# One reciprocal-root activation for Ln and Exp, and a Newton step of three operations, in a hybrid decoder block on one core

## The chip, the core and the metric

The kernel runs on one core of one Trainium2 chip. The core has five engines that run side by side, each with an in-order queue of its own: TensorE (PE: matmuls, transposes), VectorE (DVE), ScalarE (ACT: activations, copies, some DMA issues), GpSimd (POOL: here it splits weights and issues gathers) and SyncE (SP: issues the weight loads). They meet only at semaphores. The metric is the device time of one execution in microseconds, taken as the median over runs.

## The reference

One decoder block over 1024 tokens of width 1024, in float32: a root-mean-square norm, projections, retention in 4 heads with a variance norm inside each head, a short convolution, a gated merge, an expert retrieval over 16,384 experts behind a second norm, a gated per-layer input behind a third, and a final norm.

```python
def rms_norm(x, g):
    y = xf * lax.rsqrt(jnp.mean(xf * xf, axis=-1, keepdims=True) + EPS)
    return (y * g).astype(x.dtype)

def head_group_norm(y):
    mu = jnp.mean(y, axis=-1, keepdims=True)
    yc = y - mu
    return yc * lax.rsqrt(jnp.mean(yc * yc, axis=-1, keepdims=True) + EPS)

a = rms_norm(h, g_mix);  proj = a @ w_in
ret = silu(g_ret) * head_group_norm(chunkwise_retention(q, k, v))
merged = sigmoid(gate_r) * (ret @ w_ret_up) + sigmoid(gate_c) * ((cb * z) @ w_conv_up)
h = h + merged @ w_out
h = h + peer_ffn(rms_norm(h, g_ffn), ...)
h = h + sigmoid(rms_norm(h, g_ple) @ w_ple_gate) * (p @ w_ple_proj)
out = rms_norm(h, g_final)
```

## The kernel before

Activations are held transposed (channels on the 128 partitions, tokens along the free dimension). Every float32 matmul is made of three (high times high, high times low, low times high), so each operand is split: a cast gives the high half and a subtraction the low half. For weights POOL does both (`split`, L645 and L647) in the early part of the program, one pair of instructions for each weight tile of 128x1024, as soon as PE has finished the tile before the last; later ACT casts and POOL subtracts (L653). For activations ACT casts, and DVE and POOL share the subtractions.

The tokens go through the mixers in two passes: pass 0 has 384 tokens, pass 1 has 640. In each pass `mixers` runs four heads (`head`; each is six weight tiles on PE, with the work of the head before in between), a last `head` that only finishes, then the gate, convolution and merge tiles, and the output tiles. After the mixers comes the norm ahead of the query tiles (norm 1 in pass 0, norm 3 in pass 1). Norm 0 stands at the start of the program, norm 2 (pass 1's first) runs beside pass 0's query tiles. Then the experts: 128 tiles against `peer_u`, 128 groups of rows against `peer_v`, with gathered rows dotted on DVE beside them. The tail is the projection of the per-layer input (`ple_part`, 8 parts on PE), norm 4 in two halves of 512 tokens, 16 gate tiles (t = 0 to 15, `F_TILE + t`) and the final norm, half by half.

Each of the 16 roots is made alike. PE sums squares against a matrix of equal numbers into a scratch bank of PSUM (L792, L1088 in the tail), so every partition holds the mean. ACT takes Ln(mean + eps) (L1114; L1542 and L1568 in the tail) and then Exp(-0.5 x) (L1116; L1545, L1570), which is the rough root in `nt0`. DVE refines it once by Newton (`newton`; `half_rstd` in the tail): L1606 makes -0.5 (mean + eps) from the scratch bank while Exp is still to come and thereby drains the bank, L1609 squares the root, L1611 multiplies the two, L1612 adds 1.5 and multiplies by the root (L2242, L2244, L2246 and L2247 in the tail). Then the rows are scaled: L1624 for norms, L1884 and L1887 for a head, L2253 and L2278 in the tail.

Roots by place: norms 0 to 3 (4), heads of pass 0 (4), heads of pass 1 (4), norm 4 (2 halves), final norm (2 halves). In `head`, ACT's queue holds behind the root the copies of the transposed values (L1195, L1198, L1200) and the sigmoids (L1205, L1207). Ahead of norm 4's second half stands its first, and behind both stand the copies `ple_out(1)` and later (L1534), which free the PSUM banks that PE's parts 3 and later wait for:

```python
ple_out(0)
act.wait_ge(stat_filled, 5)
row_std(0)
row_std(1)
for n in range(1, 4):
    ple_out(n)
```

ACT evaluates functions from tables, and an ACT_TABLE_LOAD stands in its queue wherever the next function is not in the set that is loaded. Ln, Exp and Sigmoid each have one in front of them here.

Of the kernel before, what the change touches and what calls it, by code (L numbers as in the profile page):

```python
# [31 lines left out]
P = 128  # L32
# [10 lines left out]
EPS = 1e-6  # L43
LOWEST = -3.0e38
# [228 lines left out]
def build(nc, x_t, p_t, stream, u_rows, v_rows, key_t, gains, conv_c, rope, head_c, shape_c, out_t,  # L273
          score_d, act_d, gate_d, res_d):
    with ExitStack() as ctx:
# [35 lines left out]
        eps_t = lay("eps_t", [P, 1], F32)  # L311
        headz = lay("headz", [P, 2], F32)
# [450 lines left out]
        def _(pe):  # L763
# [65 lines left out]
            def head(h, ps, first=False):  # L829
# [24 lines left out]
                if not first:  # L854
                    pe.wait_ge(ysqsum_ready, heads)
                    column_mean(m, "var", ones_v, nt2[ps], WIDTH[ps])
# [30 lines left out]
            def mixers(ps):  # L887
# [15 lines left out]
                def variance():  # L903
                    pe.wait_ge(ysqsum_ready, HEADS * ps + HEADS)
                    column_mean(m, "var", ones_v, nt2[ps], WIDTH[ps])
# [199 lines left out]
        def _(act):  # L1105
# [6 lines left out]
            def rough_rstd(ps, slot, done, count):  # L1112

                act.activation(nt0[ps][:, :], slot[:, 0:(TS, TDN, T)[ps]], ACT.Ln, bias=eps_t[:, 0:1]).then_inc(done, 1)  # L1114
                act.wait_ge(done, count + 1)
                act.activation(nt0[ps][:, :], nt0[ps][:, :], ACT.Exp, scale=-0.5).then_inc(done, 1)  # L1116

            def norm_std(norm, ps, slot):
                act.wait_ge(stat_filled, norm + 1)
                rough_rstd(ps, scr[slot], std_done, 2 * norm)  # L1120
# [42 lines left out]
            def head(h, ps, first=False, last=False):  # L1163
# [26 lines left out]
                if not first:  # L1190
                    act.wait_ge(scr_filled, m.filled("var"))
                    rough_rstd(ps, scr[1], gstd_done, 2 * (heads - 1))
# [371 lines left out]
            def out_std(half):  # L1564
# [3 lines left out]
                act.activation(n0, scr[half][:, 0:HALF], ACT.Ln, bias=eps_t[:, 0:1]).then_inc(std_done, 1)  # L1568
                act.wait_ge(std_done, 2 * (6 + half) + 1)
                act.activation(n0, n0, ACT.Exp, scale=-0.5).then_inc(std_done, 1)  # L1570
# [19 lines left out]
        def _(dve):  # L1590
# [23 lines left out]
            def norm_rstd(norm, ps, slot):  # L1614
                newton(ps, scr[slot], std_done, 2 * norm + 2, stat_drained, norm + 1)
# [219 lines left out]
            def head(h, ps, first=False, last=False):  # L1835
# [40 lines left out]
                if not first:  # L1876
# [5 lines left out]
                    newton(ps, scr[1], gstd_done, 2 * heads, scr_drained[1], m.drained("var"))  # L1882
# [32 lines left out]
            def mixers(ps, spare):  # L1915
# [3 lines left out]
                if ps == 0:  # L1919
                    with dve.Fori(1, HEADS) as h:  # L1920
                        inside = steps.enter(h - 1, 6 + 3 + 2 + 2)
# [316 lines left out]
            def half_rstd(turn, half, mean):  # L2238
                at = slice(half * HALF, (half + 1) * HALF)
                n0, n1, n2 = nt0[2][:, at], nt1[2][:, at], nt2[2][:, at]  # L2240
                dve.wait_ge(std_done, 2 * (turn + half) + 1)
                dve.tensor_scalar(n1, mean, -0.5, -0.5 * EPS, ALU.mult, ALU.add).then_inc(stat_drained, 1)  # L2242
# [149 lines left out]
```

## Time and profile before

| | us |
|---|---|
| median of 3 runs | 3545.93 (3545.28 to 3547.4) |
| the profiled execution | 3540.74 |
| its span | 3538.9 |
| PE busy | 3391.1 (96%) |
| DVE busy | 2532.9 (72%) |
| POOL busy | 2175.7 (61%) |
| ACT busy | 1287.8 (36%) |
| mean granted share of TensorE's clock | 0.983 |

The span is the time from the first instruction to the last in one profiled execution; 1.84 us of that execution lie around it. Times in the rows are counted from the start of the span. A row of a timeline has the start, the duration, the engine, the line, the operation, output<-inputs and the shapes; in brackets stands how long the engine was idle before it and who ended that. Several instructions of one kind in a row are merged (x2, x3).

### The profile page before, as it was taken

How to read it: one execution, taken by the hardware profiler on the slowest of the kernel's cores; microseconds unless marked ns; L12 is line 12 of the kernel's file. 1: busy time of each engine (PE TensorE's matmuls, PEld its weight loads, DVE VectorE, ACT ScalarE, POOL GpSimd, SP SyncE). 2: the span in 40 equal slices, each digit the busy share in tenths (PEclk: the TensorE clock that was granted, in tenths of full speed). 3: DMA queues.
4: the chain of work that ended last, by engine and by line, in shares of the span. 5: the costliest groups of instructions: out<-in, count | busy, mean ns of one | idle time of the engine just before them, and what ended most of it. 6: DMA issues, size and time to landing. Idle time of an engine off the chain costs nothing.

```text
span 3538.9 us, 58475 instructions
## 1 busy us (share of the span) xinstructions
PE 3391.1 (96%) x22379; PEld 3332.5 (94%) x22379; DVE 2532.9 (72%) x4232; ACT 1287.8 (36%) x2013; POOL 2175.7 (61%) x1426
## 2 busy tenths in 40 slices
PE   7899989998999989999999999999999999999987
PEld 6899979988999979999999999999999999999975
DVE  5615467668887667898989899754667676767567
ACT  3310131232121232456565655653333333333242
POOL 5578865332678656566666666765566665666544
PEclk9999989999999999999999999999999999999998
DMA  4233432111589868789898988988999998999712
GB/s 153 81 116 122 136 114 79 57 50 60 184 311 316 279 218 310 252 306 335 306 331 309 328 313 311 319 299 284 337 318 334 341 321 304 320 333 320 271 48 95
DMA packets 324309, 851.18 MB, mean 241 GB/s; under 512 B 27665, under 2 KB 125457, under 8 KB 320785
## 3 DMA queue, kind: packets, MB, share of 16 engines
q0 software_dynamic: 110592, 402.70, 31.2%
q1 hardware_dynamic: 92160, 300.62, 25.6%
q10 hardware_dynamic: 121360, 145.25, 12.2%
q8 instruction: 122, 2.00, 0.2%
q14 instruction: 75, 0.61, 0.0%
HBM read 756.20 MB, written 92.27 MB: 240 GB/s over the span
## 4 chain that ended last, share of the span: by engine, by line
PE 84%; DVE 10%; ACT 2%; issue 2%; DMA 1%; POOL 1%; ACTq 0%; DVEq 0%; SPq 0%; POOLq 0%
PE main L777 53%; PE main L1037 24%; PE scr L975 4%; DMA rows<-v_rows,s_idx 1%; DVE rows L1800 1%; PE scr L875 1%; PE scr L792 1%; DVE rowb L1624 1%; PE main L1079 1%; PE scr L816 0%; DVE res L2286 0%; DVE y L1884 0%; PE scr L820 0%; DVE rowb L2010 0%; DVE rowb L1600 0%
## 5 line engine op out<-in xcount | busy, mean ns | idle before, releaser
L653 POOL TENSOR_TENSOR w_lo<-raw,w_hi 128x1024 fp32r<-128x1024 f32 x206 | 534.3, 2594 | 421.9 <-ACT w_hi L1132 417.9
L777 PE MATMUL main<-mix_hi,w_hi 128*128 128x320 f32 (+1 forms) x2816 | 685.2, 317 | 29.8 <-DVE mix_lo L1632 9.9
L777 PE MATMUL main<-mix_lo,w_hi 128*128 128x320 f32 (+1 forms) x2816 | 673.2, 313 | 0.0
L777 PE MATMUL main<-mix_hi,w_lo 128*128 128x320 f32 (+1 forms) x2816 | 673.1, 313 | 0.0
L1807 DVE SCALAR_TENSOR_TENSOR scr<-rows,s_dot,scr 128x1024 f32<-128x1024 f32 x381 | 489.0, 1284 | 167.0 <-DMA rows<-v_rows,s_idx 150.6
L777 PEld LDWEIGHTS main<-mix_hi,w_hi 128*128 128x128 f32 x2816 | 476.8, 190 | 34.5 <-issue 19.6
L777 PE MATMUL main<-a_hi,w_hi 128*128 128x320 f32 (+1 forms) x1728 | 465.8, 324 | 24.2 <-DVE a_lo L1632 8.6
L686 POOL DMA_INDIRECT rows<-u_rows,s_idx x384 | 397.4, 1035 | 135.8 <-issue 69.0
L777 PEld LDWEIGHTS main<-mix_lo,w_hi 128*128 128x128 f32 x2816 | 480.3, 189 | 0.0
L777 PEld LDWEIGHTS main<-mix_hi,w_lo 128*128 128x128 f32 x2816 | 479.5, 189 | 0.0
L1037 PE MATMUL main<-h_hi,v_hi 128*128 128x320 f32 x2048 | 467.7, 310 | 9.3 <-issue 3.5
L1800 DVE CUSTOM_DVE_ANT_0 rows<-rows,scr 128x1024 f32<-128x1024 f32 x384 | 446.1, 1215 | 41.4 <-PE main L777 22.7
L1037 PE MATMUL main<-h_lo,v_hi 128*128 128x320 f32 x2048 | 467.4, 309 | 0.0
L1037 PE MATMUL main<-h_hi,v_lo 128*128 128x320 f32 x2048 | 467.0, 309 | 0.0
L733 POOL TENSOR_TENSOR v_lo<-raw,v_hi 128x1024 fp32r<-128x1024 f32 x126 | 301.8, 2415 | 264.3 <-ACT v_hi L1429 257.9
L777 PE MATMUL main<-a_lo,w_hi 128*128 128x320 f32 (+1 forms) x1728 | 458.9, 320 | 0.0
L777 PE MATMUL main<-a_hi,w_lo 128*128 128x320 f32 (+1 forms) x1728 | 458.3, 320 | 0.0
L686 POOL DMA_INDIRECT rows<-v_rows,s_idx x384 | 368.9, 961 | 126.8 <-issue 82.9
L1037 PEld LDWEIGHTS main<-h_hi,v_hi 128*128 128x128 f32 x2048 | 342.5, 188 | 10.5 <-issue 4.0
L1037 PEld LDWEIGHTS main<-h_hi,v_lo 128*128 128x128 f32 x2048 | 343.0, 188 | 0.0
L1037 PEld LDWEIGHTS main<-h_lo,v_hi 128*128 128x128 f32 x2048 | 343.0, 188 | 0.0
L777 PEld LDWEIGHTS main<-a_hi,w_hi 128*128 128x128 f32 x1728 | 302.9, 190 | 32.6 <-issue 19.0
(270 smaller groups left out, 5137.4 us busy)
## 6 DMA issues: line engine op xcount, KB each, us to landing
raw<-stream SPq DMA_DIRECT2D x480, 512.0 KB
gate_d<-gbuf ACTq DMA_DIRECT2D x20, 2048.0 KB, 8.9
act_d<-actb ACTq DMA_DIRECT2D x120, 320.0 KB
gate_in<-gate_d ACTq DMA_DIRECT2D x30, 1280.0 KB
h<-act_d SPq DMA_DIRECT2D x120, 320.0 KB
rows<-u_rows,s_idx POOLq DMA_INDIRECT x384
rows<-v_rows,s_idx POOLq DMA_INDIRECT x384
score_d<-stage ACTq DMA_DIRECT2D x16, 320.0 KB
```

The source lines that it names most:

```text
L653: pool.tensor_tensor(w_lo[:, s, :], raw[:, s, :], w_hi[:, s, :].bitcast(F32), ALU.subtract) \
L686: pool.indirect_dma_start(rows[HOMES[k]][:, :], None, table[:, :], bass.IndirectOffsetOnAxis(ap=s_idx[:, t, n:n + 1], axis=0)) \
L733: pool.tensor_tensor(v_tile(v_lo, n), raw[:, n % 2, :], v_tile(v_hi, n).bitcast(F32), ALU.subtract).then_inc(v_split, 1)
L777: last = pe.matmul(main[s][:, dst:dst + n], wt[:, s, c * P:(c + 1) * P], rows[:, c, src:src + n], start=(c == 0 and wt is w_hi and rows is ...
L792: last = pe.matmul(slot[:, at:at + n], ones[:, :], src[:, at:at + n], start=True, stop=True)
L875: last = pe.matmul(slot[:, t * P:(t + 1) * P], qrow[ps][:, s, t * P:(t + 1) * P], row_of(keys[ps], 2 * h + s), start=True, stop=True)
L975: last = pe.matmul(scr[1][:, w * HALF + k * P:w * HALF + (k + 1) * P], hot_key(half + w, 1, k), hot_key(half + w, 0, k), start=True, stop= ...
L1037: last = pe.matmul(slot[:, half * HALF:half * HALF + HD], v_tile(vt, n)[:, col:col + P], ht[u][:, k, half * HD:(half + 1) * HD], start=(k ...
L1079: last = pe.matmul(main[s][:, half * HALF:(half + 1) * HALF], wt[:, n // 4, col:col + P], pt[:, c, half * HALF:(half + 1) * HALF], start=( ...
L1624: dve.scalar_tensor_tensor(rowb[ps][:, c % 4, :], res_row(c, ps), gain[:, which, c:c + 1], nt0[ps][:, :], ALU.mult, ALU.mult).then_inc(row ...
L1800: dve.tensor_tensor_reduce(got[:, :], got[:, :], acc[:, :], 1.0, 0.0, ALU.mult, ALU.add, s_dot[:, t, n:n + 1]).then_inc(dot_done, 1)
L1807: dve.scalar_tensor_tensor(acc[:, :], got[:, :], s_dot[:, t, n:n + 1], acc[:, :], ALU.mult, ALU.add).then_inc(dot_done, 1)
```

## The change

Ln and Exp become one activation, Abs_reciprocal_sqrt, which reads the scratch bank with a scale and a bias. The matrix of ones that sums squares now holds -1/D, so the bank holds minus the mean; the scale turns the sign back and divides by a constant (ROOT, ROOT_V for the heads) so that Newton's step needs no halving. DVE's step is then: square the root; (bank - eps) times that square, which reads the bank and drains it; add a constant and multiply by the root. The early instruction L1606 and L2242 is gone. The semaphores of the root count one for each root instead of two.

```diff
+ROOT = 0.5 ** (2 / 3)
+ROOT_V = 2.0 ** (2 / 3)
...
-                    column_mean(m, "var", ones_v, nt2[ps], WIDTH[ps])
+                    column_mean(m, "var", ones_d, nt2[ps], WIDTH[ps])
...
-            def rough_rstd(ps, slot, done, count):
-                act.activation(nt0[ps][:, :], slot[:, 0:(TS, TDN, T)[ps]], ACT.Ln, bias=eps_t[:, 0:1]).then_inc(done, 1)
-                act.wait_ge(done, count + 1)
-                act.activation(nt0[ps][:, :], nt0[ps][:, :], ACT.Exp, scale=-0.5).then_inc(done, 1)
+            def rough_rstd(ps, slot, done, eps, scale):
+                act.activation(nt0[ps][:, :], slot[:, 0:(TS, TDN, T)[ps]], ACT.Abs_reciprocal_sqrt, bias=eps[:, 0:1],
+                               scale=scale).then_inc(done, 1)
...
             def row_std(half):
                 n0 = nt0[2][:, half * HALF:(half + 1) * HALF]
-                act.activation(n0, scr[0][:, half * HALF:(half + 1) * HALF], ACT.Ln, bias=eps_t[:, 0:1]) \
-                    .then_inc(std_done, 1)
-                act.wait_ge(std_done, 2 * (4 + half) + 1)
-                act.activation(n0, n0, ACT.Exp, scale=-0.5).then_inc(std_done, 1)
+                act.activation(n0, scr[0][:, half * HALF:(half + 1) * HALF], ACT.Abs_reciprocal_sqrt,
+                               bias=eps_t[:, 0:1], scale=-1.0 / ROOT).then_inc(std_done, 1)
...
-            def newton(ps, slot, rough, rough_done, drained, value):
-                n0, n1, n2 = nt0[ps][:, :], nt1[ps][:, :], nt2[ps][:, :]
-                dve.wait_ge(rough, rough_done - 1)
-                dve.tensor_scalar(n1, slot[:, 0:(TS, TDN, T)[ps]], -0.5, -0.5 * EPS, ALU.mult, ALU.add) \
-                    .then_inc(drained, 1)
+            def newton(ps, slot, rough, rough_done, drained, value, eps, middle):
+                n0, n2 = nt0[ps][:, :], nt2[ps][:, :]
                 dve.wait_ge(rough, rough_done)
                 steps.then(dve.tensor_tensor(n2, n0, n0, ALU.mult))
+                dve.scalar_tensor_tensor(n2, slot[:, 0:(TS, TDN, T)[ps]], eps, n2, ALU.subtract, ALU.mult) \
+                    .then_inc(drained, 1)
                 dve.wait_ge(drained, value)
-                steps.then(dve.tensor_tensor(n2, n2, n1, ALU.mult))
-                steps.then(dve.scalar_tensor_tensor(n0, n2, 1.5, n0, ALU.add, ALU.mult))
+                steps.then(dve.scalar_tensor_tensor(n0, n2, middle, n0, ALU.add, ALU.mult))
...
-            dve.memset(ones_d[:, :], 1.0 / D).then_inc(ones_set, 1)
+            dve.memset(ones_d[:, :], -1.0 / D).then_inc(ones_set, 1)
...
-            dve.memset(eps_t[:, :], EPS).then_inc(ones_set, 1)
+            dve.memset(eps_v[:, :], EPS / ROOT_V)
+            dve.memset(eps_t[:, :], EPS / ROOT).then_inc(ones_set, 1)
```

`out_std` changes as `row_std` does, and `half_rstd` as `newton` does.

On DVE, at the start of the program (norm 0), before; `rowb` stands for the squares, `nt` for the root, `scr` for the bank:

```order
L1597 COPY rowb_72<-rowb_72 128x384 [waits sq_done]
L1600 TENSOR_TENSOR rowb_72<-rowb_72 128x384 [waits sq_added,sq_done] x7
L1606 TENSOR_SCALAR rowb_72<-scr 128x384 [waits std_done]
L1609 TENSOR_TENSOR rowb_72<-nt_0_71 128x384 [waits std_done]
L1611 TENSOR_TENSOR rowb_72<-rowb_72 128x384 [waits stat_drained,dve_step]
L1612 SCALAR_TENSOR_TENSOR nt_0_71<-rowb_72,nt_0_71 128x384 [waits dve_step]
L1624 SCALAR_TENSOR_TENSOR rowb_72<-res,gain,nt_0_71 128x384 [waits consts_in,dve_step]
```

The same place on DVE with the change:

```order
L1596 COPY rowb_73<-rowb_73 128x384 [waits sq_done]
L1599 TENSOR_TENSOR rowb_73<-rowb_73 128x384 [waits sq_added,sq_done] x7
L1605 TENSOR_TENSOR rowb_73<-nt_0_72 128x384 [waits std_done]
L1606 SCALAR_TENSOR_TENSOR rowb_73<-scr,rowb_73 128x384 [waits dve_step]
L1609 SCALAR_TENSOR_TENSOR nt_0_72<-rowb_73,nt_0_72 128x384 [waits stat_drained]
L1621 SCALAR_TENSOR_TENSOR rowb_73<-res,gain,nt_0_72 128x384 [waits consts_in,dve_step]
```

The instruction that read the bank ahead of the root is gone; the bank is now read second, behind the square.

On ACT, around norm 4, before (`ple` is the per-layer projection, copied out of PSUM):

```order
L1534 COPY ple<-main 128x1024 [waits ple_filled]
L1542 ACT_TABLE_LOAD
L1542 ACTIVATE nt_2_81<-scr,eps_t 128x512 [waits stat_filled]
L1545 ACT_TABLE_LOAD
L1545 ACTIVATE nt_2_81<-nt_2_81 128x512 [waits std_done]
L1542 ACT_TABLE_LOAD
L1542 ACTIVATE nt_2_81<-scr,eps_t 128x512
L1545 ACT_TABLE_LOAD
L1545 ACTIVATE nt_2_81<-nt_2_81 128x512 [waits std_done]
L1534 COPY ple<-main 128x1024 [waits ple_filled] x2
```

The same place on ACT with the change:

```order
L1536 COPY ple<-main 128x1024 [waits ple_filled]
L1544 ACT_TABLE_LOAD
L1544 ACTIVATE nt_2_82<-scr,eps_t 128x512 [waits stat_filled]
L1544 ACTIVATE nt_2_82<-scr,eps_t 128x512
L1536 COPY ple<-main 128x1024 [waits ple_filled] x2
```

Between the first copy and the next, four table loads and four activations become one load and two activations.

## Rows read from the trace of the kernel before

**Rows 1.** The page: busy time by engine, and the chain that ended last, by engine.

```profile
PE 3391.1 (96%) x22379; PEld 3332.5 (94%) x22379; DVE 2532.9 (72%) x4232; ACT 1287.8 (36%) x2013; POOL 2175.7 (61%) x1426
...
PE 84%; DVE 10%; ACT 2%; issue 2%; DMA 1%; POOL 1%; ACTq 0%; DVEq 0%; SPq 0%; POOLq 0%
```

**Rows 2.** Waits of PE over the program: us in total, times, longest us.

```profile
PE main L777 <- DVE mix_lo L1632: 9.9, 3, 8.8
...
PE main L777 <- DVE mix_lo L1832: 8.0, 2, 5.5
...
PE scr L875 <- ACTq L1299: 1.6, 3, 0.7
```

**Rows 3.** Groups on ACT, by shape: count | busy us, mean ns.

```profile
L1114 ACT ACT_TABLE_LOAD x12 | 15.4, 1283 | 0.6 <-issue 0.4
L1116 ACT ACT_TABLE_LOAD x12 | 15.4, 1283 | 0.2
...
L1116 ACT ACTIVATE nt<-nt 128x640 f32<-128x640 f32 x6 | 4.4, 738 | 0.1
```

**Rows 4.** Timeline of ACT at norm 1: start us, us, instruction.

```profile
456.47 1.28 ACT L1116 ACT_TABLE_LOAD   x1
...
457.77 0.52 ACT L1116 ACTIVATE nt<-nt 128x384 f32<-128x384 f32 x1
```

**Rows 5.** Timeline of DVE at norm 1.

```profile
456.49 0.56 DVE L1606 TENSOR_SCALAR rowb<-scr 128x384 f32<-128x384 f32 x1 [2.41 <-ACT nt L1114]
458.32 0.56 DVE L1609 TENSOR_TENSOR rowb<-nt 128x384 f32<-128x384 f32 x1 [1.28 <-ACT nt L1116]
```

**Rows 6.** Timeline of POOL at norm 0.

```profile
11.84 2.34 POOL L647 TENSOR_TENSOR w_lo<-raw,w_hi 128x1024 fp32r<-128x1024 f32 x1
...
15.24 2.63 POOL L647 TENSOR_TENSOR w_lo<-raw,w_hi 128x1024 fp32r<-128x1024 f32 x1
```

**Rows 7.** Timeline of DVE at norm 0.

```profile
13.28 0.56 DVE L1606 TENSOR_SCALAR rowb<-scr 128x384 f32<-128x384 f32 x1 [2.42 <-ACT nt L1114]
...
15.71 2.58 DVE L1611 TENSOR_TENSOR rowb<-rowb 128x384 f32<-128x384 f32 x1
```

**Rows 8.** Timeline of POOL in pass 0, second head.

```profile
78.04 2.39 POOL L647 TENSOR_TENSOR w_lo<-raw,w_hi 128x1024 fp32r<-128x1024 f32 x1
82.07 1.04 POOL L645 CAST w_hi<-raw 128x1024 fp32r<-128x1024 f32 x1 [1.64 <-PE main L777]
```

**Rows 9.** Timeline of DVE in the same head.

```profile
78.05 0.56 DVE L1606 TENSOR_SCALAR rowb<-scr 128x384 f32<-128x384 f32 x1 [3.86 <-ACT nt L1114]
79.89 0.95 DVE L1609 TENSOR_TENSOR rowb<-nt 128x384 f32<-128x384 f32 x1 [1.28 <-ACT nt L1116]
...
82.15 1.37 DVE L1884 TENSOR_TENSOR y<-y,nt 128x384 f32<-128x384 f32 x1
```

**Rows 10.** Timeline of POOL in pass 0's last head.

```profile
172.60 1.04 POOL L645 CAST w_hi<-raw 128x1024 fp32r<-128x1024 f32 x1 [12.44 <-PE main L777]
```

**Rows 11.** Timeline of DVE in pass 0's last head.

```profile
171.09 0.56 DVE L1606 TENSOR_SCALAR rowb<-scr 128x384 f32<-128x384 f32 x1 [0.30 <-ACT nt L1114]
...
174.09 2.59 DVE L1611 TENSOR_TENSOR rowb<-rowb 128x384 f32<-128x384 f32 x1
...
179.42 1.03 DVE L1832 TENSOR_TENSOR mix_lo<-res,mix_hi 128x384 fp32r<-128x384 f32 x2
```

**Rows 12.** Timeline of PE: two moments at which it had waited.

```profile
661.28 0.38 PE L777 MATMUL main<-a_hi,w_hi 128*128 128x320 f32 x1 [2.90 <-DVE g L1894]
...
3400.09 0.79 PE L1079 MATMUL main<-p_hi,p_whi 128*128 128x512 f32 x1 [2.69 <-ACT ple L1534]
```

**Rows 13.** Windows behind the second: us, PE busy (instructions), granted clock, DMA.

```profile
3400.10:3403.50 3.40, 3.40 (x9) 0.53 0.03 5
3403.50:3415.40 11.90, 11.90 (x54) 1.00 0.00 0
```

**Rows 14.** Timeline of DVE in the tail, gate tile 11.

```profile
3505.47 2.76 DVE L2246 TENSOR_TENSOR rowb<-rowb 128x512 f32<-128x512 f32 x1
```

More of the change, by code:

```diff
@@ L311, in build @@
         eps_t = lay("eps_t", [P, 1], F32)
+        eps_v = lay("eps_v", [P, 1], F32)
         headz = lay("headz", [P, 2], F32)
@@ L904, in variance @@
                     pe.wait_ge(ysqsum_ready, HEADS * ps + HEADS)
-                    column_mean(m, "var", ones_v, nt2[ps], WIDTH[ps])
+                    column_mean(m, "var", ones_d, nt2[ps], WIDTH[ps])
                 def of_a(pair, s, **more):
@@ L1110, in square @@
                 act.activation(sqb[ps][:, c % 2, :], src, ACT.Square).then_inc(sq_done, 1)
-            def rough_rstd(ps, slot, done, count):
-                act.activation(nt0[ps][:, :], slot[:, 0:(TS, TDN, T)[ps]], ACT.Ln, bias=eps_t[:, 0:1]).then_inc(done, 1)
-                act.wait_ge(done, count + 1)
-                act.activation(nt0[ps][:, :], nt0[ps][:, :], ACT.Exp, scale=-0.5).then_inc(done, 1)
+            def rough_rstd(ps, slot, done, eps, scale):
+                act.activation(nt0[ps][:, :], slot[:, 0:(TS, TDN, T)[ps]], ACT.Abs_reciprocal_sqrt, bias=eps[:, 0:1],
+                               scale=scale).then_inc(done, 1)
             def norm_std(norm, ps, slot):
                 act.wait_ge(stat_filled, norm + 1)
-                rough_rstd(ps, scr[slot], std_done, 2 * norm)
+                rough_rstd(ps, scr[slot], std_done, eps_t, -1.0 / ROOT)
             def hi_rows(dst, norm, ps):
@@ L1191, in head @@
                     act.wait_ge(scr_filled, m.filled("var"))
-                    rough_rstd(ps, scr[1], gstd_done, 2 * (heads - 1))
+                    rough_rstd(ps, scr[1], gstd_done, eps_v, -(D // DV) / ROOT_V)
                 if not last:
@@ L1567, in out_std @@
                 act.wait_ge(stat_filled, 6 + half)
-                act.activation(n0, scr[half][:, 0:HALF], ACT.Ln, bias=eps_t[:, 0:1]).then_inc(std_done, 1)
-                act.wait_ge(std_done, 2 * (6 + half) + 1)
-                act.activation(n0, n0, ACT.Exp, scale=-0.5).then_inc(std_done, 1)
+                act.activation(n0, scr[half][:, 0:HALF], ACT.Abs_reciprocal_sqrt, bias=eps_t[:, 0:1],
+                               scale=-1.0 / ROOT).then_inc(std_done, 1)
             for t in range(2 * DC):
@@ L1881, in head @@
                         lo_of(ps, DC, mix_lo[ps], mix_hi[ps], range(1, 4))
-                    newton(ps, scr[1], gstd_done, 2 * heads, scr_drained[1], m.drained("var"))
+                    newton(ps, scr[1], gstd_done, heads, scr_drained[1], m.drained("var"), EPS * DV / D, 0.75 * ROOT_V)
                     for e in range(2):
@@ L1920, in mixers @@
                     with dve.Fori(1, HEADS) as h:
-                        inside = steps.enter(h - 1, 6 + 3 + 2 + 2)
+                        inside = steps.enter(h - 1, 6 + 2 + 2 + 2)
                         head(h, ps)
@@ L2239, in half_rstd @@
                 at = slice(half * HALF, (half + 1) * HALF)
-                n0, n1, n2 = nt0[2][:, at], nt1[2][:, at], nt2[2][:, at]
-                dve.wait_ge(std_done, 2 * (turn + half) + 1)
-                dve.tensor_scalar(n1, mean, -0.5, -0.5 * EPS, ALU.mult, ALU.add).then_inc(stat_drained, 1)
-                dve.wait_ge(std_done, 2 * (turn + half) + 2)
+                n0, n2 = nt0[2][:, at], nt2[2][:, at]
+                dve.wait_ge(std_done, turn + half + 1)
                 steps.then(dve.tensor_tensor(n2, n0, n0, ALU.mult))
+                dve.scalar_tensor_tensor(n2, mean, EPS, n2, ALU.subtract, ALU.mult).then_inc(stat_drained, 1)
                 dve.wait_ge(stat_drained, turn + half + 1)
-                steps.then(dve.tensor_tensor(n2, n2, n1, ALU.mult))
-                steps.then(dve.scalar_tensor_tensor(n0, n2, 1.5, n0, ALU.add, ALU.mult))
+                steps.then(dve.scalar_tensor_tensor(n0, n2, 3 * ROOT, n0, ALU.add, ALU.mult))
             def half_row(half, c):
```

2 lines of the change are left out of this document (1 added, 1 removed).

## The prediction

> **What bounds the kernel now.** I read the page first: PE is busy 96% of the span and makes 84% of the chain that ended last, ACT is busy 36% and makes 2% [rows 1]. So work taken from ACT is worth nothing in itself; it is worth what PE waits for a root. The waits of PE say where that is: 8.8 us at norm 3 before the first low half of a row, 5.5 and 2.5 us (8.0 in two waits) at the last head of each pass, and little where the roots run beside other tiles: 1.6 us in three waits for the copies of key scores, behind which norm 2 sits in ACT's queue [rows 2]. The rest is to follow a root from ACT through DVE to PE at each of its 16 places, in timelines.
>
> **What the change takes off the path.** ACT loads a table before each Ln and again before each Exp: 12 and 12 times on the lines of norms 0 to 3 and the heads, 1.28 us each [rows 3]. The load before Ln stays, as a load before the new activation, and mostly runs while ACT waits for the mean. The one between Ln and Exp lies on the path. At norm 1 it takes 1.28 us and Exp 0.52, with 0.03 between them [rows 4], and DVE shows the whole: it could start at 456.49, when Ln was done, and squares the root only at 458.32 [rows 5]. That is 1.83 us for 384 tokens. For 640 tokens Exp is 0.74 [rows 3], so 2.05; for a half of 512 tokens, in between, about 1.94.
>
> The new activation is not in the trace. It reads the same bank with a bias, as Ln does, so I give it Ln's time; an activation of this trace that would cost nothing or twice as much moves each place by at most 0.6 to 0.8 us, which is the bound from both sides.
>
> On DVE the three operations behind the root stay three. The early one, 0.56, goes; but it ran beside the table load, so it was free [rows 5]. In its place the bank is read by the second operation. Bank readers cost the same 0.56 as the others [rows 5], so Newton's length is unchanged where nothing disturbs it.
>
> **What gives time back: POOL.** At norm 0 POOL works on a weight from 11.84 to 14.18 and from 15.24 to 17.87 [rows 6]. DVE's product of two SBUF operands that starts at 15.71 takes 2.58 instead of 0.56 and ends 0.42 behind POOL; the bank reader at 13.28, inside POOL's first stretch, takes 0.56 [rows 7]. So a DVE operation with two inputs in SBUF waits out POOL's instruction, and one that reads the bank does not. The Trainium skill has the same rule (SBUF — State Buffer, Who interferes with whom): the pair of ports is locked by whoever issues first, and DVE takes it when both inputs are in SBUF. By that rule, the trace agrees; the change makes one of the three operations immune, and moves the others to other moments of POOL's pattern, which PE sets and the change does not.
>
> **Place by place.**
> Norm 0. The square would start at 13.28, inside POOL's first stretch, and end at 14.6; the bank reader follows freely to 15.2; the last operation waits for POOL's cast and ends near 15.8; the first row then waits for POOL's second stretch, which DVE has pushed to about 18.0, and ends at 18.5 instead of 19.5. Gain 1.1 (bounds 0 and 1.83).
>
> Heads of pass 0, first three roots (one loop, one pattern). Ln's end frees DVE at 78.05, and POOL has begun its subtraction at 78.04, until 80.43 [rows 8]. The square, which started at 79.89 and ended at 80.84 because of POOL [rows 9], would start at 78.05 and end at 80.84 all the same. Then two operations as before, and the scaling of y again meets POOL's cast of 82.07 [rows 8] at 82.15 [rows 9]. Gain 0, three times; bounds 0 and 1.8 each.
>
> Last head of pass 0. PE's next tile does not finish until POOL's cast at 172.60 [rows 10]. From 171.09 on there is room for the square, the bank reader and nearly the last operation, against a product that now starts at 174.09 and is held for 2.59 [rows 11]. But both scalings of y are then held by POOL in turn (until about 174.2 and 176.9), and the low half on which PE waits starts at 178.0, not 179.42 [rows 11]. Gain 1.4 of a wait of 5.5.
>
> Norm 1 has no POOL in its way: 1.8. Norm 3 likewise: 2.1, out of the 8.8 of wait. Last head of pass 1 likewise: 2.1 of its 2.5. Norm 2 runs beside tiles; I take 0.4 (bounds 0 and the 1.6 of those waits).
>
> Heads of pass 1. The square meets POOL again, so the step gains 0.4 and the rows behind it about 1.3, after which DVE sorts scores, with small operations that POOL holds or not by a hair. In the first of these heads PE waits 2.90 for the gate product behind the sorting [rows 12]. It may get back 0.2 or 2.3; I take 1.0. In the other two the wait follows a sigmoid that PE itself sets: 0.
>
> Norm 4. Both halves stand on ACT between `ple_out(0)` and `ple_out(1)`: four loads and four activations, 7.8 us, and PE's part 3 waits 2.69 for that copy [rows 12]. With one load and two activations ACT is done 5 us sooner, which is more than the wait, so the wait goes whole; next late is PE itself. And behind the wait PE runs at a granted clock of 0.53: 9 matmuls in 3.40 us, where the next 54 take 11.90, 0.22 each [rows 13]. That is about 1.2 GHz for a stretch after idling, and costs another 3.40 - 9 x 0.22 = 1.4. Edge counts in the windows make this a low figure. Gain 4.4 (bounds 2.7 and 4.7).
>
> Final norm. The first half sits inside gate tile 11, on a chain of sigmoid, product, sum, square and Newton's step. ACT gives 1.9. On DVE POOL held the product of the step for 2.76 [rows 14] instead of 0.69; without it the square will be held by the same instruction of POOL, and the product behind by the next. Stepping through it leaves 2.1 (bounds 0 and 4.7). The second half is the end of the program, with POOL done: 1.9.
>
> **Sum.** 1.1 + 0 + 1.4 + 1.8 + 0.4 + 1.0 + 2.1 + 2.1 + 4.4 + 2.1 + 1.9 = 18.3 us. The profiled execution took 3540.74 (span 3538.9 and 1.84 around it), so 3522.4 for it. The median of the runs is 5.2 above that execution; taken along, 3545.9 - 18.3 = 3527.6, which is 0.5% less.
>
> The Trainium skill (ScalarE: Activation LUTs, What ACT_TABLE_LOAD costs) adds a drain of some 1.38 us to each change of set. By it every place on the path would give 1.4 more, about 11 in all. The rows speak against it: between load and Exp there are 0.02 us [rows 4].
>
> **Rivals.**
> The stalls fall better (a). If DVE got the pair ahead of POOL in the heads, where they start within 0.01 to 0.03 us of each other [rows 8, 9], the scaling would slip in before the cast and each of six heads would give 1 to 1.7; with more short stretches of full clock, some 8 us more: 3520. For it: the near tie. Against: POOL is first. 12%.
>
> The tail pays less (b). Norm 4's wait is followed at once by another (its rows on DVE and POOL), or gate tile 11 loses its gain to POOL: 4.4 + 2.1 become 2 and 0, and the start nothing: 18.3 - 5.6 = 12.7 gained, 3533. For it: DVE and POOL are nearly as full there as PE. 17%.
>
> Hidden anyway (c). If PE's waits ended at something else than the root in most places, under 7 us would be left: 3540 to 3547. Against: the chain passes through the root at norms 0, 1, 3, 4 and the end. 3%.
>
> Slower (d). The bank is now drained by the second operation, behind the held square: near 81.5 instead of 78.61 (78.05 + 0.56) [rows 9]. PE needs this bank for the next transposes, when the tile is done whose end lets POOL's cast start at 82.07 [rows 8], so about 81.9. The margin shrinks from 3.3 us to 0.4. Were the drain held through POOL's next pair, to about 86.8, PE would wait 4.9 in each of six heads, 29 us: against 17 elsewhere that ends 12 slower, 3558. It decides from 2.9 us of lateness a head. Against: a bank reader is not held, and in pass 1 the margin is over 3 us. 1%.
>
> The change is as it says: the rows of order show the loads gone. A new activation dearer than Ln by more than 1.9 us would undo it; 1%.
>
> **Numbers.** My forecast (3523 to 3532) has 66%, (a) 12, (b) 17, (c) 3, (d) and a dear activation 2. Likeliest: 3527.6. The range 3519 to 3535.5 takes in (a) and most of (b), and holds 8 in 10. A measurement of this kernel can tell 0.2%, 7.1 us, from no change: faster by more 94%, within it 4%, slower by more 2%.
>
> **What would show it.** Table loads on the root's line 12, none on an Exp; DVE's square at norm 1 about 0.03 behind the new activation. In the second head of pass 0 the square should still end 0.4 behind POOL's subtraction; if it is short there, (a) holds. At norm 4 no wait of PE on `ple`, and no stretch of half clock behind it. The last Newton step should end 1.9 sooner after the last mean. I am wrong if the new activation takes longer than Ln, if a second load stands by it, or if PE shows a new wait on `scr` for the transposes in `head`.

## The result, and the profile after

On the chip of the first measurement the kernel after took 3516.0 us (median of 4, 3513.3 to 3518.4) against 3546.7 (3545.3 to 3548.9): a ratio of 0.9917, 95% interval 0.9905 to 0.9929. The forecast was 3527.6 and the fast end of its range 3519.0: faster, as forecast, but by 27 to 31 us where 18 were expected. The profiled execution took 3513.3 (span 3511.4) where the one of before took 3540.7: 27.4 less.

The page after, busy time and chain, for [rows 1]:

```profile
PE 3381.9 (96%) x22379; PEld 3324.0 (95%) x22379; DVE 2526.4 (72%) x4217; ACT 1254.7 (36%) x1979; POOL 2180.1 (62%) x1426
...
PE 81%; DVE 12%; DMA 2%; ACT 2%; issue 2%; POOL 1%; ACTq 0%; DVEq 0%; SPq 0%; POOLq 0%
```

Waits of PE after (us in total, times, longest), for [rows 2]. The longest of norm 3 went from 8.8 to 6.8; the last heads from 8.0 in two waits to 4.4; the copies behind norm 2 from 1.6 to 0.7:

```profile
PE main L780 <- DVE mix_lo L1629: 8.2, 3, 6.8
...
PE main L780 <- DVE mix_lo L1830: 4.4, 2, 4.0
...
PE scr L878 <- ACTq L1301: 0.7, 1, 0.7
```

ACT's groups by shape after, for [rows 3]. The 24 loads on the two lines of the root became 11 on one, and the new activation takes 583 ns for 384 tokens, where Ln took 582:

```profile
L1117 ACT ACT_TABLE_LOAD x11 | 14.1, 1283 | 0.6 <-issue 0.4
L1117 ACT ACTIVATE nt<-scr,eps_v 128x640 f32<-128x640 f32 x4 | 3.2, 797 | 21.3 <-PE scr L795 21.3
...
L1117 ACT ACTIVATE nt<-scr,eps_v 128x384 f32<-128x384 f32 x4 | 2.3, 583 | 10.7 <-PE scr L795 10.7
```

The forecast had 12 loads. The missing one is norm 2's: its activation follows ACT's copy with no load in front. Between the roots of norms 1 and 2 ACT runs only squares, casts and copies, and none of them has a load. Before, there were two loads at this place:

```profile
498.80 0.80 ACT L1117 ACTIVATE nt<-scr,eps_t 128x640 f32<-128x640 f32 x1
```

```profile
509.24 1.28 ACT L1114 ACT_TABLE_LOAD   x1
...
511.35 1.28 ACT L1116 ACT_TABLE_LOAD   x1
```

DVE at norm 1 after, for [rows 5]. The square starts 0.03 behind the root, and nothing is left of the 1.83:

```profile
448.87 0.56 DVE L1605 TENSOR_TENSOR rowb<-nt 128x384 f32<-128x384 f32 x1 [2.42 <-ACT nt L1117]
449.46 0.56 DVE L1606 SCALAR_TENSOR_TENSOR rowb<-scr,rowb 128x384 f32<-128x384 f32 x1
450.06 0.56 DVE L1609 SCALAR_TENSOR_TENSOR nt<-rowb,nt 128x384 f32<-128x384 f32 x1
```

ACT at norm 4 after. One load and two activations; the copy for which PE waited 2.69 [rows 12] now waits for PE instead:

```profile
3372.74 1.28 ACT L1544 ACT_TABLE_LOAD   x1
3374.03 1.27 ACT L1544 ACTIVATE nt<-scr,eps_t 128x512 f32<-128x512 f32 x2
3376.19 1.02 ACT L1536 COPY ple<-main 128x1024 f32<-128x1024 f32 x1 [0.89 <-PE main L1082]
```

**Where the time went.** PE's 22,379 matmuls come in the same order in all kernels here, so the lead of a kernel is the start of a matmul in the profile of before less its start in its own. A growing lead is time that PE has gained. Gain by place, from two profiles of the kernel after:

| place | forecast | after | again |
|---|---|---|---|
| norm 0, behind its mean | 1.1 | 0.5 | 0.6 |
| pass 0, heads 1 to 3 | 0 | 3.5 | 3.5 |
| pass 0, last head | 1.4 | 1.9 | 1.4 |
| norm 1 | 1.8 | 2.6 | 2.5 |
| norm 2 | 0.4 | 1.7 | 1.7 |
| pass 1, heads | 1.0 | 2.7 | 2.6 |
| pass 1, last head | 2.1 | 0.7 | 0.6 |
| norm 3 | 2.1 | 1.8 | 1.8 |
| up to 1500 us | 0 | 0.9 | 0.9 |
| norm 4 and gate tiles behind | 4.4 | 4.5 | 4.5 |
| final norm, first half | 2.1 | 2.6 | 2.5 |
| final norm, second half | 1.9 | 1.9 | 1.9 |
| sum | 18.3 | 25.3 | 24.6 |

The sums are of the gains before rounding. In the first profile another 0.8 came before the first mean (input arrived sooner), 0.9 at 37 us and 0.4 between 1500 and 3385 us; none of them is the change's (see the repeats). The largest miss is the three looped heads, the first three roots of pass 0, which one loop makes. POOL and then DVE in pass 0's second head after, for [rows 8, 9]:

```profile
75.77 2.39 POOL L650 TENSOR_TENSOR w_lo<-raw,w_hi 128x1024 fp32r<-128x1024 f32 x1
79.81 1.45 POOL L648 CAST w_hi<-raw 128x1024 fp32r<-128x1024 f32 x1 [1.64 <-PE main L780]
```

```profile
75.79 2.79 DVE L1605 TENSOR_TENSOR rowb<-nt 128x384 f32<-128x384 f32 x1 [3.87 <-ACT nt L1117]
78.61 0.56 DVE L1606 SCALAR_TENSOR_TENSOR rowb<-scr,rowb 128x384 f32<-128x384 f32 x1
79.21 0.56 DVE L1609 SCALAR_TENSOR_TENSOR nt<-rowb,nt 128x384 f32<-128x384 f32 x1
79.80 1.87 DVE L1882 TENSOR_TENSOR y<-y,nt 128x384 f32<-128x384 f32 x2
```

The square ends at 78.58, 0.41 behind POOL's subtraction, exactly as forecast. But the scaling of y now starts at 79.80, 0.01 ahead of POOL's cast; before, it started at 82.15, 0.086 behind the cast at 82.07. Both scalings take 1.87 in place of 4.03, and the cast is the one that is stretched (1.45 for 1.04). PE's wait behind it:

```profile
85.98 0.45 PE L780 MATMUL main<-a_hi,w_hi 128*128 128x384 f32 x1 [0.55 <-DVE g L1892]
```

Before, that wait was:

```profile
89.39 0.44 PE L777 MATMUL main<-a_hi,w_hi 128*128 128x384 f32 x1 [1.69 <-DVE g L1894]
```

Why 0.1 sooner? Before, the square [rows 9] ended at 80.842 and the product started at 80.965, 0.123 later:

```profile
80.97 0.56 DVE L1611 TENSOR_TENSOR rowb<-rowb 128x384 f32<-128x384 f32 x1
```

Everywhere outside the loop that gap is 0.034 or 0.035. The new step has one wait behind each operation, and its register operations run while DVE computes. That is theory T; its rival R is that the copies behind the root on ACT leave sooner.

### The profile page after: what moved, and what is told of

It reads as the page before. It is cut to its first block, busy times and chain, and to the rows that moved or that the text cites. A ratio compares the mean times of both kernels' runs of the same rounds, so it can differ in the third digit from the quotient of the medians.

```text
span 3511.4 us, 58404 instructions
## 1 busy us (share of the span) xinstructions
PE 3381.9 (96%) x22379; PEld 3324.0 (95%) x22379; DVE 2526.4 (72%) x4217; ACT 1254.7 (36%) x1979; POOL 2180.1 (62%) x1426
## 4 chain that ended last, share of the span: by engine, by line
PE 81%; DVE 12%; DMA 2%; ACT 2%; issue 2%; POOL 1%; ACTq 0%; DVEq 0%; SPq 0%; POOLq 0%
PE main L780 52%; PE main L1040 21%; PE scr L978 4%; DMA rows<-v_rows,s_idx 1%; DVE rows L1798 1%; POOL v_lo L736 1%; PE scr L878 1%; DVE res L2282 1%; PE main L1082 1%; PE scr L795 1%; DVE rowb L1621 1%; DVE scr L1805 1%; DVE fg L2281 1%; DVE rowb L1605 1%; DVE rowb L2285 1%
```

## Experiments

Gains are read from the lead of PE: from 54 us (behind the start and the tie at 37 us) to 1500, and from 3385.5 to the end. Each ratio is to the kernel before on the same chip. The two profiles of before differ by 0.3 and 1.8 in the last two columns, the three of the kernel after (e1 counted, for the reason below) by 2.4 and 0.1; smaller differences than these are not told apart.

| kernel | ratio to before (95%) | 54 to 1500 | tail |
|---|---|---|---|
| after | 0.9917 (0.9905 to 0.9929) | 15.8 | 9.0 |
| after, again | 0.9918 (0.9904 to 0.9931) | 15.1 | 8.9 |
| before, again | 1.0001 (0.9992 to 1.0010) | 0.3 | 1.8 |
| e1, wait asked again | 0.9921 (0.9908 to 0.9935) | 17.5 | 9.0 |
| e2, before, wait moved | 0.9990 (0.9981 to 0.9999) | 5.2 | 0.0 |
| e3, DVE's part alone | 0.9978 (0.9969 to 0.9987) | 7.2 | 1.2 |
| e4, new activation, four operations | 0.9939 (0.9925 to 0.9952) | 13.1 | 8.5 |
| e5b, fresh wait | 0.9952 (0.9933 to 0.9971) | 8.9 | 9.2 |
| e6b, ACT squares | 0.9911 (0.9890 to 0.9933) | 19.7 | 9.2 |
| e7b, before, two orders | 0.9981 (0.9967 to 0.9995) | 2.5 | 3.4 |
| e8, gate first | 0.9886 (0.9870 to 0.9901) | 32.2 | 12.6 |

**e1_second_wait.**

```diff
                 steps.then(dve.tensor_tensor(n2, n0, n0, ALU.mult))
+                dve.wait_ge(rough, rough_done)
                 dve.scalar_tensor_tensor(n2, slot[...
```

> The kernel after, with one more wait in front of the bank reader of Newton's step; its semaphore has long been reached, but in the loop over pass 0's heads each wait takes its value from a register, so the step gets one more register operation there (about 0.09 us, as the kernel before had between its square and its product: 0.123 us where an unrolled place has 0.034). Nothing else changes; in unrolled places the wait should be free. Theory T (the near tie): DVE's first scaling of y again starts about 0.08 behind POOL's cast in the three heads, waits out the subtraction behind the cast, and PE again waits 1.7 us for the gate product in heads 1 and 2 (0.55 in the kernel after) and 3.7 at the third (2.6): about 3.3 us lost for 0.27 us of register operations, so 3516.6 where the kernel after had 3513.3. Rival R (the heads gain because the root leaves ACT sooner, so that the copies behind it on ACT are sooner): nothing is lost beyond 0.3.

3517.1 (3510.4 to 3517.7), which by the time alone would have passed for theory T's 3516.6. But in its trace the gap in the loop stayed at 0.034, the scaling 0.01 ahead of the cast and PE's waits short: the experiment failed to make its own condition. Its trace has no register operation behind the square, so the value of a wait just asked for was still at hand. It decides nothing between T and R, and serves as a repeat of the kernel after.

**e2_wait_moved.** The kernel before, the wait put where DVE idles.

```diff
+                dve.wait_ge(drained, value)
                 dve.wait_ge(rough, rough_done)
                 steps.then(dve.tensor_tensor(n2, n0, n0, ALU.mult))
-                dve.wait_ge(drained, value)
```

> The kernel before, Ln and Exp and its four operations on DVE kept; only the wait for the drained bank moves from behind the square to ahead of it, where DVE is idle anyway. In the loop each DVE operation of the step then has one wait behind it instead of two. Theory T: the product follows the square by 0.034 instead of 0.123, the first scaling starts at 82.064 where POOL's cast starts at 82.067, wins the pair of ports by 3 ns, and the three heads give their 3.3 us to the kernel before: about 3537.4 by the profiled execution's 3540.7. With a margin of 3 ns it may also fall on the other side, and then nothing is gained. Rival R: 0.0 to 0.3 gained.

DVE, then POOL, in the second head:

```profile
81.06 0.56 DVE L1612 SCALAR_TENSOR_TENSOR nt<-rowb,nt 128x384 f32<-128x384 f32 x1
81.65 1.87 DVE L1884 TENSOR_TENSOR y<-y,nt 128x384 f32<-128x384 f32 x2
```

```profile
81.66 1.45 POOL L645 CAST w_hi<-raw 128x1024 fp32r<-128x1024 f32 x1 [1.64 <-PE main L777]
```

The scaling is 0.01 ahead, and PE's lead grows by 1.16, 1.18 and 1.18 in the three heads: 3.5 us with Ln, Exp and all four operations in place. R falls. Of this the median shows only 2.5 us (0.1%). In the profiled execution the last head gave 1.3 back, stretches at a higher clock near 470 and 730 us gave 2.8, and 6.9 were lost between 1500 and 3385 us, where no experiment changes anything.

**e3_three_ops_ln_exp.** ACT's root as Ln and Exp again, with the new scale and bias:

```diff
-                ... ACT.Abs_reciprocal_sqrt, bias=eps[:, 0:1], scale=scale).then_inc(done, 1)
+                ... ACT.Ln, bias=eps[:, 0:1], scale=scale).then_inc(done, 1)
+                act.wait_ge(done, count + 1)
+                ... ACT.Exp, scale=-0.5).then_inc(done, 1)
```

> The kernel after, but Ln and Exp (with the same scale and bias) in place of the new activation at all 16 roots: DVE's half of the change alone. Theory T: on DVE one wait behind each operation, so the heads of pass 0 give the 3.3 us by themselves, and everything else stays as before: about 3537.4. Rival R: the heads' gain comes with the activation, so 3540 to 3541. By both, norms 0, 1, 3 and 4 and the final norm give nothing here.

The three heads gave 3.5 here too, norm 1's first wait, norm 3 and norm 4's wait nothing. So all of the gain in the looped heads comes without the new activation.

**e4_four_ops_one_act.** The new activation with four operations on DVE; the bank is copied out by an operation of its own behind the root. The waits are rewritten too, one behind each operation, so this is not the kernel before with ACT's half added.

```diff
+                dve.tensor_scalar(n1, slot[...], eps, 1.0, ALU.subtract, ALU.mult).then_inc(drained, 1)
+                dve.wait_ge(drained, value)
                 steps.then(dve.tensor_tensor(n2, n0, n0, ALU.mult))
-                dve.scalar_tensor_tensor(n2, slot[...], eps, n2, ALU.subtract, ALU.mult).then_inc(drained, 1)
-                dve.wait_ge(drained, value)
+                steps.then(dve.tensor_tensor(n2, n2, n1, ALU.mult))
```

> The kernel after with ACT's half of the change alone: the new activation, but Newton's step on DVE in four operations, the bank copied out by the first of them once the root is there. Adds 0.59 us (384 tokens) to 0.86 (640) at each root on the path: norm 0, norm 1, norm 3, the last head of each pass and the two final halves, about 5 us in all by the trace's spacings, at norm 4 nothing, and in pass 0's heads nothing by theory T, since the bank reader runs under POOL's subtraction and the scaling follows with the same spacing: 3518 to 3519 against 3513.3. Rival R says the same here except that it gives no reason for the heads to keep or lose theirs.

The heads kept 3.5 with one wait behind each operation. PE's wait at norm 1 was shortened by 1.2, where the kernel after shortened it by 1.8, and that at norm 3 by 1.2 for 2.05: the extra operation is the difference. Against the three profiles of the kernel after (e1 counted) it lost 2.1 to 4.4 in the mixers and 0.4 to 0.5 in the tail, where 5 were forecast; the medians of e4 and e1, on one chip, are 5.7 apart.

**e5b_fresh_wait.** The kernel after with a wait whose value must be worked out, in the three looped heads alone.

```diff
                 steps.then(dve.tensor_tensor(n2, n0, n0, ALU.mult))
+                if fresh is not None:
+                    dve.wait_ge(drained, fresh)
...
+                           m.drained("var") - 1 if ps == 0 and not last else None)
```

> The kernel after with one more wait between the square and the bank reader in the three looped heads of pass 0, this time for a value that the loop has to work out anew (the last wait asked for again had its register ready, and cost nothing). The wait itself has long been met; it puts one register operation behind the square's end. Theory T (near tie): the bank reader follows the square by about 0.12 instead of 0.034, the first scaling of y starts some 0.08 behind POOL's cast instead of 0.009 ahead, is held by cast and subtraction in turn, and PE waits 1.7 in heads 1 and 2 and 3.7 at the third (0.55 and 2.6 in the kernel after): 3.5 us lost by the end of the heads for three register operations. Rival: the three heads lose 0.1 each.

DVE, POOL and PE in the second head:

```profile
77.07 2.79 DVE L1605 TENSOR_TENSOR rowb<-nt 128x384 f32<-128x384 f32 x1 [3.86 <-ACT nt L1117]
79.99 0.56 DVE L1608 SCALAR_TENSOR_TENSOR rowb<-scr,rowb 128x384 f32<-128x384 f32 x1
80.58 0.56 DVE L1611 SCALAR_TENSOR_TENSOR nt<-rowb,nt 128x384 f32<-128x384 f32 x1
81.18 4.03 DVE L1885 TENSOR_TENSOR y<-y,nt 128x384 f32<-128x384 f32 x2
```

```profile
81.08 1.04 POOL L648 CAST w_hi<-raw 128x1024 fp32r<-128x1024 f32 x1 [1.64 <-PE main L780]
```

```profile
88.41 0.44 PE L780 MATMUL main<-a_hi,w_hi 128*128 128x384 f32 x1 [1.69 <-DVE g L1895]
```

The gap is 0.13 by these rounded rows (79.86 to 79.99), the scaling 0.09 behind the cast, the wait 1.69 again, and the heads' gain is gone: leads of 0.98, 0.97, 0.96 and 0.96 through the three. By 1500 us the kernel has gained 8.9, against 15.1 to 17.5 for the kernel after: three delays of 0.1 cost 6.2 to 8.6 us, 3.5 of them in the heads, the rest behind them. T holds in both directions: e2 takes the second wait out of the kernel before and gains 3.5, e5b puts one into the kernel after and loses them.

**e6b_act_squares.**

```diff
                 act.activation(dst, src, ACT.Abs_reciprocal_sqrt, bias=eps[:, 0:1], scale=scale).then_inc(done, 1)
+                act.wait_ge(done, count + 1)
+                act.activation(square, dst, ACT.Square).then_inc(done, 1)
...
-                steps.then(dve.tensor_tensor(n2, n0, n0, ALU.mult))
```

> The kernel after, with the square of the rough root made by ACT, right behind the root (0.03 apart, 0.50 to 0.74 long by ACT's other squares), so DVE's step has two operations left and its first reads the bank. Nobody holds ACT. Theory P (a DVE operation with both inputs in SBUF waits out POOL's instruction): in each of the three looped heads the bank reader no longer starts at POOL's end but about 0.55 behind the root, only the last operation waits for POOL's subtraction, and the scaling starts about 1.15 sooner, well ahead of the cast: PE's 0.55 go in heads 1 and 2 and up to 1.1 in the third; norm 0 gives about 1.3 on the step; in pass 1's heads the step is 1.6 sooner and PE's 0.55 in its first head go; elsewhere 0.04 to 0.12 a root. In all 3 to 5 us less than the kernel after by 1500 us of the span. Rival: the square on ACT only moves the hold to the next two-input operation and nothing reaches PE: within 1 us of the kernel after.

DVE and POOL in the second head, then in the third:

```profile
76.79 0.56 DVE L1613 SCALAR_TENSOR_TENSOR rowb<-scr,rowb 128x384 f32<-128x384 f32 x1 [4.41 <-ACT rowb L1119]
77.38 1.65 DVE L1616 SCALAR_TENSOR_TENSOR nt<-rowb,nt 128x384 f32<-128x384 f32 x1
79.06 1.03 DVE L1889 TENSOR_TENSOR y<-y,nt 128x384 f32<-128x384 f32 x2
80.25 1.87 DVE L1892 TENSOR_TENSOR res<-y,g 128x384 f32 x2 [0.17 <-DVE y L1889]
...
113.15 4.12 DVE L1892 TENSOR_TENSOR res<-y,g 128x384 f32 x2 [0.17 <-DVE y L1889]
```

```profile
76.22 2.39 POOL L650 TENSOR_TENSOR w_lo<-raw,w_hi 128x1024 fp32r<-128x1024 f32 x1
...
80.25 1.47 POOL L648 CAST w_hi<-raw 128x1024 fp32r<-128x1024 f32 x1 [1.64 <-PE main L780]
...
113.14 1.04 POOL L648 CAST w_hi<-raw 128x1024 fp32r<-128x1024 f32 x1 [1.64 <-PE main L780]
```

Theory P holds: the bank reader runs through POOL's subtraction unheld, the last operation ends 0.42 behind it, and each head gives 0.8 to 0.9 more than the kernel after. These two heads are a tie at its narrowest: the product starts 3 ns behind the cast in the one and takes 1.87 with its fellow; in the other it starts 6 ns behind and the two take 4.12. In the mixers 2.2 to 4.6 us less than the kernel after; 3509.5 by the median.

**e7b_two_orders.** The kernel before with e2's move, and one copy between the halves of norm 4:

```diff
             row_std(0)
+            ple_out(1)
             row_std(1)
-            for n in range(1, 4):
+            for n in range(2, 4):
```

> The kernel before, Ln and Exp and four operations kept, with two waits put elsewhere: the heads' wait as in the run with the moved wait, and at norm 4 the copy ple_out(1) between the two halves' roots on ACT's queue instead of behind both. If norm 4's gain is one of queue order, PE's wait of 2.7 for that copy goes, and with it the stretch of half clock behind it: 2.7 to 4.2 us less between 3395 and 3450, beside the 3.5 of pass 0's heads, and the kernel before is 7 to 8 us faster without any change to a root. If PE's wait at norm 4 needs the shorter root itself, 0 to 1 there: the second half's rows then come some 1 us later, which could give it back in the gate tiles.

PE's wait of 2.69 at norm 4 is gone: 3.2 us there, as in the kernel after, with four loads still in the queue. The clock behind it was 1.00, which gave another 1.24, but then PE waited for the next copy, which stands behind the second half's root:

```profile
3406.11 0.70 PE L1079 MATMUL main<-p_hi,p_whi 128*128 128x512 f32 x2 [0.96 <-ACT ple L1534]
```

That took 1.1 back, and the tail gave 3.4 in all. The heads gave their 3.5 again and the clock took 1.2 back near 690 us. 3534.7 against 3542.4, and not the 7 to 8 us forecast.

**e8_gate_first.** ACT squares, and y times the gate is made before the root is there.

```diff
                         .then_inc(ysqsum_ready, 1)
+                    for e in range(2):
+                        steps.mark(dve.tensor_tensor(y[ps][:, e, :], y[ps][:, e, :], g[ps][:, e, :], ALU.mult))
...
-                        steps.mark(dve.tensor_tensor(y[ps][:, e, :], y[ps][:, e, :], nt0[ps][:, :], ALU.mult))
-                    settled()
-                    for e in range(2):
-                        dve.tensor_tensor(res_row(2 * (h - 1) + e, ps), y[ps][:, e, :], g[ps][:, e, :], ALU.mult) \
+                        dve.tensor_tensor(res_row(2 * (h - 1) + e, ps), y[ps][:, e, :], nt0[ps][:, :], ALU.mult) \
```

> The kernel in which ACT squares, and in a head y is multiplied by the gate g before the root is there, while DVE waits for it (it sits idle 3.86 us there in the kernel before), instead of behind the scaling: two operations are left behind the root instead of four. By theory P the two early products run into POOL's cast at worst, and the rows are ready about 1.1 sooner in pass 0 (more where products were held by POOL), 1.6 in pass 1. Of this PE waited for little in the looped heads (0 left in heads 1 and 2, 1.8 at the third), about 4 us at the last head of pass 0 and 0.4 at the last of pass 1: 2 to 3 us less than with ACT's squares alone by 1500 us of the span. Rival: the early products are held by POOL's subtraction and make the bank reader late: 0 or a loss of up to 2.7 a head.

DVE in the second head. The products run in idle time, and the rows are done by 80.26:

```profile
72.34 1.02 DVE L1886 TENSOR_TENSOR y<-y,g 128x384 f32<-128x384 f32 x2
76.82 0.56 DVE L1613 SCALAR_TENSOR_TENSOR rowb<-scr,rowb 128x384 f32<-128x384 f32 x1 [3.46 <-ACT rowb L1119]
77.41 1.65 DVE L1616 SCALAR_TENSOR_TENSOR nt<-rowb,nt 128x384 f32<-128x384 f32 x1
79.23 1.03 DVE L1891 TENSOR_TENSOR res<-y,nt 128x384 f32 x2 [0.17 <-DVE nt L1616]
```

3501.5 (3499.2 to 3505.5), the fastest of all: 1.1% under before, and 13 us under the kernel after, whose repeat ran on the same chip (3514.9). Far more than the 2 to 3 forecast beyond e6b: the last head of pass 0 gave 2.5 more with the clock behind it, and the third head of pass 1 3.0 (a wait of PE of 2.74 in e6b is gone). Between 200 and 480 us e6b falls back by some three us and e8 does not, and three more come in the tail, both where nothing was changed; those I did not separate.

**after_again and before_again.**

> The kernel after, unchanged, for the spread of one kernel and beside the two others on the same chip. By the theory of near ties its three looped heads have the same spacings to 0.01 us (scaling 0.010 ahead of POOL's cast, PE's waits 0.55, 0.55 and 2.6), since they hang on PE's own tiles; at 37 us, where DVE's product started 0.001 ahead of a cast in the first profile and 0.045 behind it in the run with the free wait, it may fall either way, 0.9 us apart; and between 1500 and 3300 us, where PE waits for gathered rows, executions differ by several us.

> The kernel before, unchanged: a second profile. Its three looped heads should show PE's waits of 1.7, 1.7 and 3.7 again (the scaling 0.08 behind POOL's cast), and the same rows at norms 1, 3 and 4 to 0.1 us; what differs should lie at the start (0.4 to 0.8 by the arrival of the input) and between 1500 and 3300 us.

The heads repeat to 0.03 us in both kernels. At 37 us the second profile of before gained 0.89 by itself. There a product of the first head meets a cast in another tie: it starts 1 ns ahead of it in the first profile of after, 2 ns behind it in the second of before, and 6 to 45 ns behind it in the ten other profiles, which lose it. The kernels do not differ there, so it hangs on something like the arrival of the input, which no run separates. Between 1500 and 3385 us the two profiles of after gained 0.4 and 0.2 on the first of before, the second of before lost 4.8, and e5b lost 13.3. The largest part is one place, where PE waits for the one-hot rows of the gathering stage: not at all in the first profile of before, nor in those of after, e1 and e6b; 3.2 to 3.4 us in before's second profile, e2, e3, e4 and e8; and over 7 in e7b and e5b:

```profile
2192.52 0.58 PE L978 MATMUL scr<-hot 128*128 128x128 f32 x1 [7.24 <-ACT hot L1397]
```

So executions can be 5 to 13 us apart by what no kernel here changed, and the leads, not the times, tell the experiments apart.

## Why the prediction was wrong

The direction, the chain and most places stood; the time fell outside the range. The step that failed is the 0 for the three looped heads of pass 0. The median came 11.6 us under the forecast: 7.0 in the places of the table, 2.1 that are not the change's (the input, the tie at 37 us, the gathering stage), and 2.5 because the median lies 2.7 above the profiled execution and not 5.2. Without what e5b takes away, 6.2 us or more, the median would have been inside the range.

- **Heads of pass 0: failed.** The step "then two operations as before, and the scaling of y again meets POOL's cast" assumed that two operations keep their spacing when the waits between them are rewritten. The diff shows two waits becoming one, and the trace of before showed a spacing of 0.123 (79.89 + 0.95 = 80.84, next 80.965) against 0.034 elsewhere. With a margin of 0.086 in [rows 8, 9] that was the number to look at. Gain 3.5 for 0, and with what follows 6.2 to 8.6 of the total: e5b, which undoes only this, gains 8.9 in the mixers where the forecast had 8.8 for the same places without norm 0.
- **Rival (a)** named the near tie but gave a wrong reason ("DVE got the pair ahead of POOL" at the root) and 12%. What flipped is the scaling, by its waits. Its 3520 was still 4 us too high.
- **The square held by POOL**: right, 0.41 behind it. **Newton's length, and the new activation at Ln's price**: right, 583 ns for 582.
- **Norms 1 and 3, the last head of pass 1, norm 4, the end**: at these waits the lead grew by 1.83, 2.05, 2.04, 2.85 and 1.94, where 1.8, 2.1, 2.1, 2.7 and 1.9 were expected.
- **Norm 0: a size.** 0.5 and 0.6 for 1.1. As forecast, the first row waited for POOL's second stretch (15.22 to 17.75 in the first profile); why it then came later behind its mean than worked out, I did not follow.
- **The clock behind norm 4: right by luck.** The wait and the half clock behind it [rows 13] gave 4.5 for 4.4. But the half clock is not bound to the wait. The second profile of before has the same wait of 2.69, and behind it

```profile
3403.60:3407.00 3.40, 3.40 (x15) 1.00 0.02 5
```

where the first has 9 matmuls at 0.53 (e2 has 8 at 0.51, e3 8 at 0.50). The columns are the window, its length, PE's busy time, the granted clock, DMA's share and GB/s. Measured from that second profile the kernel after gained 2.8 here, no more than the wait.
- **Norm 2: a size, and a premise.** 1.7 for 0.4. Three waits of PE lost 0.53, 0.53 and 0.61. "The load before Ln stays" did not hold here: both loads went, and the root takes 0.80 of ACT's queue where it took 4.14. In e2 the same stretch gave nothing, in e3 (new operations on DVE, old root) 0.6, and in e4 (new root, one operation more) 1.0. The gain lies just above the upper bound of 1.6.
- **Pass 1's first head: a size.** "0.2 or 2.3; I take 1.0": the wait of 2.90 fell to 0.55, 2.36. The gate product was behind the root, not behind the sorting. e2 and e3 gained nothing there, e4 2.36, so it is the activation.
- **The clock.** I counted it at norm 4 alone. Before and after, the same matmuls (some 446) of pass 1's heads, then the tile behind the last head:

```profile
662.00:733.00 71.00, 67.10 (x446) 65.31 (x445) 53.13 (x174) 13.60 (x17) 24.47 (x14) 0.95 0.19 61
...
809.20:816.00 6.80, 6.80 (x36) 6.80 (x37) 6.39 (x33) 0.00 (x0) 2.15 (x1) 0.75 0.48 154
```

```profile
647.00:718.00 71.00, 66.01 (x447) 64.15 (x448) 54.60 (x177) 11.57 (x15) 25.52 (x15) 0.98 0.20 62
...
792.40:799.20 6.80, 6.80 (x30) 6.80 (x31) 6.46 (x29) 0.00 (x0) 2.18 (x1) 0.60 0.50 154
```

The columns are the window, its length, PE's busy time, loads, DVE, ACT, POOL, the granted clock, DMA's share and GB/s. In the first pair the kernel after does the same work in 1.1 less busy time at a clock of 0.98 for 0.95; but within this window PE then waits 1.00 for DVE (L1907), where before it did not, so the lead keeps little of it. In the second PE has just waited (2.54 before, 4.06 after) and gets 30 matmuls done instead of 36: 1.4 of the last head's 2.04 were given back. So with a shortened wait a stretch near half clock, the lower of the two levels of 1.2 and 2.4 GHz, can go or come. What decides which, these runs do not show: at 480 us e2, e3 and e7b gained 1.2 to 1.4 with norm 1 unchanged.
- **Rivals (b), (c), (d)** did not come. The bank's later drain cost PE no wait.

The Trainium skill (SBUF — State Buffer, Who interferes with whom) says that the shared pair of ports is an exclusive lock and that the order of issue, not the shape of the operation, decides who blocks. The trace agrees to a few ns: in all 12 profiles here, operations of 384 elements with both inputs in SBUF that start up to 3 ns behind POOL's cast take 0.56, those 6 to 93 ns behind it 1.36 to 1.45.

## What to carry to other kernels

Where two engines share a port, read the spacing of their starts before the durations: a margin under 0.1 us is to be treated as open, and every instruction, wait or register value between is part of the sum. In a loop, put a wait on a computed value where the engine idles anyway, and never a second one behind a result that is on the path. And look for waits of queue order first: with the old root, two moved lines (e7b) gave 3.5 us in the heads and 3.4 at norm 4 (1.7 against the second profile of before), and a product moved ahead of the root (e8) gave 5.5 us beyond e6b at places that it touches.

## What the hardware showed that I had not expected

- In this loop, a second wait behind an operation of DVE costs 0.089 us (a gap of 0.123 for 0.034; 0.096 in e5b) when its value has to be computed, and nothing when the same value was asked for just before.
- The race for the shared pair turned between 3 and 6 ns behind POOL's start. If DVE wins, POOL's cast takes 1.45 to 1.47 for 1.04; if it loses, DVE's operation takes 1.37 for 0.56 and the next 2.75.
- ACT's Square behind the new activation had no table load of its own and took 0.53; with Ln and Exp each had one of 1.28 in front [rows 3]. The Trainium skill (ScalarE: Activation LUTs, Table sets: the hidden batching unit) names a set with both exp and ln, so one load should do; no run here shows such a program.
- The same program's executions differ by up to 18 us (before, 3534.7 to 3552.3 on one chip). Its two profiles differ by 1.9 in all, and the largest single difference, 3.3 us, is PE's wait for the one-hot rows in the stage with gathered rows; the tail went the other way by 1.8, 1.4 of it the clock behind norm 4.
